# Layer 2's key scores from products of weights and keys; part of these, and the readout's lag products, placed in the wait for the scan

## The reference

```python
q = (hb @ w_q).reshape(PEER_BLOCK, PEER_HEADS, 2, PEER_DHALF)
s = jnp.einsum("nhkd,hkmd->nhkm", q, sub_keys)      # 8 heads, 2 halves, 128 keys
s_half, i_half = lax.top_k(s, PEER_TOPK)
cand = s_half[:, :, 0, :, None] + s_half[:, :, 1, None, :]
top_s, top_c = lax.top_k(cand.reshape(...), PEER_TOPK)
...
g = jax.nn.softmax(top_s, axis=-1)
act = jax.nn.gelu(jnp.einsum("nd,nhkd->nhk", hb, ue))
return jnp.einsum("nhk,nhkd->nd", g * act, ve)
```

## Time and profile before

| | |
|---|---|
| time, median of 3 runs | 3846.15 us (3845.73 to 3854.15) |
| the profiled execution's own time | 3855.96 us |
| its span, from first to last instruction | 3854.2 us |
| PE busy | 3751.7 us, 97% |
| VectorE busy | 2966.6 us, 77% |
| ScalarE busy | 1590.8 us, 41% |
| GpSimd busy | 115.9 us, 3% |
| TensorE's granted clock, mean | 0.99 of full |
| DMA | 669.5 MB, mean 174 GB/s |

### The profile page before, as it was taken

The page is one execution under the profiler, slowest core; times in us unless marked ns, Lnnn a source line. Parts: engine busy times, 40 slices in busy tenths (PEclk is TensorE's granted clock), DMA queues, the critical chain, the costliest instruction groups (busy, mean ns, idle before and its releaser), DMA issues.

```text
span 3854.2 us, 61506 instructions
## 1 busy us (share of the span) xinstructions
PE 3751.7 (97%) x21356; PEld 3172.9 (82%) x21356; DVE 2966.6 (77%) x5358; ACT 1590.8 (41%) x2440; POOL 115.9 (3%) x153
## 2 busy tenths in 40 slices
PE   8999999999999999999999999999989999999998
PEld 7897799556988888888888888888768888888887
DVE  7533275896898899999887899998566997777776
ACT  6301052232137444444484444444332194444443
POOL 0000000000000000000000000000400000000000
PEclk9999999999999999999999999999999999999999
DMA  5314464475422655555515777777735415555554
GB/s 197 104 50 151 145 202 151 162 227 188 164 90 83 204 193 193 197 191 192 188 56 196 239 237 236 239 239 238 171 122 178 161 63 197 189 191 190 191 190 153
DMA packets 204274, 669.52 MB, mean 174 GB/s; under 512 B 36000, under 2 KB 46288, under 8 KB 202592
## 3 DMA queue, kind: packets, MB, share of 16 engines
q1 hardware_dynamic: 159936, 577.31, 45.3%
q0 software_dynamic: 19872, 80.86, 6.8%
q10 hardware_dynamic: 24320, 9.37, 0.9%
HBM read 639.21 MB, written 27.21 MB: 173 GB/s over the span
## 4 chain that ended last, share of the span: by engine, by line
PE 88%; DVE 9%; ACT 1%; DMA 1%; issue 1%; SPq 0%; DVEq 0%; ACTq 0%; POOLq 0%
PE psum L1116 27%; PE psum L1102 16%; PE psum L1104 9%; PE psum L736 5%; PE psum L1195 5%; PE psum L761 4%; PE psum L676 4%; PE psum L1290 3%; PE psum L1081 2%; PE psum L1386 2%; PE psum L1184 2%; DVE arena L2462 1%; DVE arena L2463 1%; PE psum L1161 1%; DVE arena L2464 1%; PE psum L1488 1%
## 5 line engine op out<-in xcount | busy, mean ns | idle before, releaser
L1116 PE MATMUL psum<-v_split,coef_split 128*128 128x512 f32 x4284 | 1034.1, 390 | 0.0
L1102 PE MATMUL psum<-input_split,u_split 128*128 128x512 f32 x2800 | 987.0, 391 | 0.0
L1116 PEld LDWEIGHTS psum<-v_split,coef_split 128*128 128x128 f32 x4284 | 779.7, 188 | 157.1 <-issue 1.2
L1104 PE MATMUL psum<-input_split,u_split 128*128 128x256 f32 x2800 | 788.9, 282 | 0.0
L1102 PEld LDWEIGHTS psum<-input_split,u_split 128*128 128x128 f32 x2800 | 525.3, 188 | 112.7
L1104 PEld LDWEIGHTS psum<-input_split,u_split 128*128 128x128 f32 x2800 | 528.5, 189 | 16.2
L1794 ACT ACTIVATE work<-work 128x256 f32<-128x256 f32 x350 | 146.7, 419 | 851.2 <-DVE work L2604 851.2
L1577 ACT ACTIVATE v_split<-ring 128x1024 fp32r<-128x1024 f32 x357 | 379.7, 1063 | 234.8 <-PE psum L1116 229.0
L2599 DVE TENSOR_TENSOR u_split<-ring,u_split 128x1024 fp32r<-128x1024 f32 x377 | 459.7, 1219 | 12.4 <-ACT u_split L1577 12.4
L2604 DVE TENSOR_REDUCE work<-psum 128x256 f32<-128x512 f32 x350 | 242.1, 692 | 258.8 <-PE psum L1104 257.5
L2599 DVE TENSOR_TENSOR v_split<-ring,v_split 128x1024 fp32r<-128x1024 f32 x357 | 433.9, 1216 | 2.3 <-ACT v_split L1577 2.3
(11 more groups left out here) (466 smaller groups left out, 4722.9 us busy)
## 6 DMA issues: line engine op xcount, KB each, us to landing
ring<-in_u SPq DMA_DIRECT2D x384, 512.0 KB, 3.3
ring<-in_v SPq DMA_DIRECT2D x384, 512.0 KB, 3.3
ring<-in_w SPq DMA_DIRECT2D x324, 512.0 KB, 3.4
arena<-in_ada POOLq DMA_DIRECT2D x48, 512.0 KB, 4.4
scratch_inj<-stage ACTq DMA_DIRECT2D x16, 512.0 KB, 5.2
arena<-scratch_inj POOLq DMA_DIRECT2D x7, 1024.0 KB, 7.8
scratch_cm<-work POOLq DMA_DIRECT2D x8, 512.0 KB, 6.4
scratch_cm<-arena POOLq DMA_DIRECT2D x8, 512.0 KB, 4.9
```

The lines of the kernel that those rows point to most:

```text
L1102: mm(bank(b), rows[:, 0, P * k:P * k + P], HR[:, k, :, :], start=(k == 0), stop=False, skip_group_check=True)
L1104: last = mm(bank(b)[:, 0:S], rows[:, 1, P * k:P * k + P], HR[:, k, 0, :], start=False, stop=(k == 7), skip_group_check=True)
L1116: last = mm(bank(2 + 2 * i + f), CFR[:, b, c, P * i:P * i + P], parts[:, v, 512 * f:512 * f + 512], start=(first and c == 0 and v == 0), s ...
```

## The change: what it does

- The stream has `wk_scan` (12 slots of the transposed query weights) ahead of `ssm_out`, and `wk_last` (20 slots) in place of `q1`. The keys come as one table, `keys2`.
- In the scan wait TensorE makes six "units" (two slots by the keys of one half of a head: 16 products), the units of heads 0 to 2. Of each, ScalarE copies the high part to `WKHO` (in place of `coef_split`) and stores it in HBM; TensorE subtracts it in PSUM (`less_high`: a product with minus the identity, `MINUS`), and ScalarE copies what is left, the low part, to `WKLO` and stores it. There is one buffer for each part. ScalarE's copies of states come behind the six units in its list.
- The readout's 64 lag products come ahead of the wait for "scanned", and `keep_busy(12, 4)` in place of `keep_busy(44, 4)`.
- In `peer_last` the queries and `keys` go. Units 6 and 7 are made ahead of the wait for the split inputs, units 8 to 15 between the scores of heads 1 to 4; the scores are three products of parts, as in layer 1. ScalarE makes both parts of these units (`last_keys`), in three sets of buffers. POOL's queue loads `keys2` and brings the six parked units back, ahead of parking X.
- Fills: 64 and 9 before the builds, then one per build and two at every fourth. ScalarE's copies of the first sums of the experts move from builds 8 and 18 to builds 2 and 12.
- Some semaphores are merged under one name ("exp_args", "rows_made"), with no other effect.

```diff
-                  ("wq", 32), ("ssm_in", 8), ("ssm_out", 16), ("q1", 40)):
+                  ("wq", 32), ("ssm_in", 8), ("wk_scan", 2 * NSCAN), ("ssm_out", 16),
+                  ("wk_last", 32 - 2 * NSCAN)):
...
+            def heads_back(h):
+
+                for kk in range(2):
+                    for part in range(2):
+                        pool.dma_start((LASTL if part else LASTH)[h][:, :, P * kk:P * kk + P].bitcast(F32),
+                                       io["wk"][2 * h + kk, part].rearrange("p (k m) -> p k m", k=KD_))\
+                            .then_inc(sem("wk_back"), 16)
+                pool.wait_ge(sem("wk_back"), 64 * h + 64)
+
+            pool.wait_ge(sem("high_parked"), 16 * NSCAN)
+            pool.wait_ge(sem("low_parked"), 16 * NSCAN)
+            pool.wait_ge(sem("y_summed"), 2)
+            pool.dma_start(KT.rearrange("p n d m -> p (n d m)"), io["keys2"]).then_inc(sem("tables_loaded"), 16)
+            heads_back(0)
+            pool.wait_ge(sem("inputs_scaled"), 5 * KD_ + 1)
+            heads_back(1)
+            heads_back(2)
...
+            def unit(n, keys, off):
+
+                for d in range(2):
+                    arrived(L.slots)
+                    for t in range(8):
+                        last = mm(PS(off + P * t, P), ring[:, L.slots % RING, P * t:P * t + P], keys[:, d, :],
+                                  start=(d == 0 and t % 4 == 0), stop=(d == 1), skip_group_check=True)
+                        if t == 0:
+                            last.then_inc(sem("slot_begun"), 1)
+                    L.slots += 1
+                L.mark(last, "scores_made")
...
+            def less_high(n, high, off):
+
+                pe.wait_ge(sem("wk_copied"), 2 * NH + n + 1)
+                for f in range(2):
+                    last = mm(bank(off // 512 + f), MINUS, high[f], start=False, stop=True, skip_group_check=True)
+                L.mark(last, "scores_made")
...
+                def made(h):
+
+                    for n in (2 * h, 2 * h + 1):
+                        if n >= NSCAN + 2:
+                            pe.wait_ge(sem("wk_low"), 2 * NH + n - 1)
+                        unit(n, KT[:, n], place(n))
+
+                def less(h):
+
+                    for n in (2 * h, 2 * h + 1):
+                        w = LASTH[h % 3][:, :, P * (n % 2):P * (n % 2) + P]
+                        less_high(n, (w[:, 0:4, :], w[:, 4:8, :]), place(n))
+
+                def last_scores(h):
+
+                    if h < NSCAN // 2:
+                        pe.wait_ge(sem("wk_back"), 64 * h + 64)
+                    else:
+                        pe.wait_ge(sem("wk_low"), 2 * NH + 2 * h + 2)
                     if h >= 2:
                         L.take("key_scores_used")
-                    arrived(L.slots)
-                    for k in range(2):
-                        for i in range(2):
-                            for d in range(2):
-                                last = mm(bank(2 + 4 * (h % 2) + i)[:, P * k:P * k + P],
-                                          QT[:, 4 * h + 2 * k + d, P * i:P * i + P],
-                                          ring[:, L.slots % RING, P * (2 * k + d):P * (2 * k + d) + P],
-                                          start=(k == 0 and d == 0), stop=(d == 1), skip_group_check=True)
-                                if k == 0 and i == 0 and d == 0:
-                                    last.then_inc(sem("slot_begun"), 1)
-                    L.slots += 1
+                    for i in range(2):
+                        for k in range(8):
+                            for x, w in ((0, LASTH), (0, LASTL), (1, LASTH)):
+                                last = mm(bank(2 + h % 2)[:, S * i:S * i + S], HR[:, k, x, P * i:P * i + P],
+                                          w[h % 3][:, k, :], start=(i == 0 and k == 0 and not x and w is LASTH),
...
-                for t in range(4 * NH):
-                    pe.wait_ge(sem("lin_free"), l0 + max(t - 1, 0))
-                    arrived(L.slots)
-                    for k in range(8):
-                        if t == 0:
-                            L.take("inputs_shifted")
-                        last = mm(bank(t % 2)[:, 0:S], ring[:, L.slots % RING, k * P:k * P + P], HT[:, k, :],
-                                  start=(k == 0), stop=(k == 7))
-                        if k == 0:
-                            last.then_inc(sem("slot_begun"), 1)
-                    last.then_inc(sem("lin_ready"), 1)
-                    L.slots += 1
-                    if t and t % 4 == 0:
-                        keys(t // 4 - 1)
-                keys(NH - 1)
-                L.lin += 4 * NH
+                pe.wait_ge(sem("tables_loaded"), 128)
+                evacuated()
+                made(3)
+                keep_busy(3, 6)
+                L.take("input_parts")
+                for h in range(NH):
+                    last_scores(h)
+                    if 1 <= h <= 5:
+                        less(h + 2)
+                    if 1 <= h <= 4:
+                        made(h + 3)
                 beside = up_ahead(2)
-                fill(beside, 32)
+                fill(beside, 64)
                 for _ in range(2):
                     L.take("key_scores_used")
-                fill(beside, 12)
                 turn_choice(KK)
                 fill(beside, 9)
                 L.take("chosen_evacuated")
                 for n in range(32):
                     build(64 + n, n % 2, n < 2)
-                    fill(beside, 1 if n % 3 == 2 else 2 if n < 31 else 8)
+                    fill(beside, 2 if n % 4 == 3 else 1)
...
-            keep_busy(44, 4)
+            for n in range(NSCAN):
+                if n >= 2:
+                    pe.wait_ge(sem("wk_low"), 2 * NH + n - 1)
+                pe.wait_ge(sem(f"keys_loaded{n % 2}"), 16 * (n // 2) + 16)
+                unit(n, SCANK[n % 2], 2048 + 1024 * (n % 2))
+                if n:
+                    less_high(n - 1, (WKHO[:, 0:512], WKHO[:, 512:1024]), 2048 + 1024 * ((n - 1) % 2))
+            less_high(NSCAN - 1, (WKHO[:, 0:512], WKHO[:, 512:1024]), 2048 + 1024 * ((NSCAN - 1) % 2))
+            pe.wait_ge(sem("wk_low"), 2 * NH + NSCAN - 1)
+            pe.wait_ge(sem("toep_loaded"), 16 * 32)
+            readout = lambda e, g, j: PS(1024 * e + P * g, P)[NCH * j:NCH * j + NCH, :]
+            for e in range(2):
+                for g in range(8):
+                    for j in range(4):
+                        q = 4 * e + j
+                        mm(readout(e, g, j), UG[:, 8 * q + g, NCH:], TOEP[:, 8 * q + g].rearrange("p t c -> p (t c)"),
+                           start=(g % 4 == 0), stop=False, skip_group_check=True)
+            keep_busy(12, 4)
             L.take("scanned")
...
-                    for part in range(3):
+                    for part in range(2):
                         for j in range(4):
                             q = 4 * e + j
-                            o = PS(1024 * e + P * g, P)[NCH * j:NCH * j + NCH, :]
-                            if part == 0:
-                                mm(o, UG[:, 8 * q + g, NCH:], TOEP[:, 8 * q + g].rearrange("p t c -> p (t c)"),
-                                   start=(g % 4 == 0), stop=False, skip_group_check=True)
-                            else:
-                                last = mm(o, HS[:, :, part - 1, 8 * q + g], BATCHES[8 + q][0][:, g, part - 1, :],
-                                          start=False, stop=(part == 2), skip_group_check=True)
+                            last = mm(readout(e, g, j), HS[:, :, part, 8 * q + g], BATCHES[8 + q][0][:, g, part, :],
+                                      start=False, stop=(part == 1), skip_group_check=True)
...
+            def last_keys(h):
+
+                act.wait_ge(sem("key_scores"), NH + h - 2)
+                for n in (2 * h, 2 * h + 1):
+                    L.take("scores_made")
+                    copy(LASTH[h % 3][:, :, P * (n % 2):P * (n % 2) + P], PS(0 if n % 2 else 2048, 8, P))\
+                        .then_inc(sem("wk_copied"), 1)
+                for n in (2 * h, 2 * h + 1):
+                    L.take("scores_made")
+                    copy(LASTL[h % 3][:, :, P * (n % 2):P * (n % 2) + P], PS(0 if n % 2 else 2048, 8, P))\
+                        .then_inc(sem("wk_low"), 1)
...
+            def scan_unit(n):
+
+                o = 2048 + 1024 * (n % 2)
+                act.wait_ge(sem("scores_made"), 3 * NH + (2 * n if n else 1))
+                if n:
+                    act.wait_ge(sem("high_parked"), 16 * n)
+                copy(WKHO, PS(o, D)).then_inc(sem("wk_copied"), 1)
+                act.wait_ge(sem("wk_copied"), 2 * NH + n + 1)
+                act.dma_start(io["wk"][n, 0], OUTS[0]).then_inc(sem("high_parked"), 16)
+                if n + 2 < NSCAN:
+                    scan_keys(n + 2)
+                act.wait_ge(sem("scores_made"), 3 * NH + min(2 * n + 3, 2 * NSCAN))
+                if n:
```

(6 more changed lines are left out.)

104 lines of the change are left out of this document (51 added, 53 removed).

## The result

The changed kernel takes 3864.92 us in the median of 6 runs (3862.00 to 3868.98), the kernel before 3850.24 in 6 (3845.73 to 3854.15): ratio 1.0037, 95% interval 1.0026 to 1.0047. It is **slower by 0.37%**, some 14 us; the forecast was 3841.3 us in a range to 3856.

A forecast was written before the change was run, and what follows sets the result against it. TensorE was taken to set the time over the whole span, with three waits that matter. Terms -6.8 - 2.9 + 2.0 + 0 + 1.8 + 1.0 = -4.9 us, from 3846.15 to 3841.3 us; likely 3834 to 3848, range 3830 to 3856.

The forecast's parts named there:

- Part 1: Start of layer 2's choice: queries and their scores go, first scores at 2942.8 against 2949.68; -6.8 us.
- Part 2: Heads of the choice: VectorE sets the pace and only its idle goes, 6 gaps of 0.49; -2.9 us.
- Part 3: After the last head: TensorE waits for the chosen keys, then transposes and first build come slower; +2.0 us.
- Part 4: Builds of the gates: twenty fills fewer, 8.7 us of TensorE time, priced at nothing because ScalarE covers it.
- rival B: Builds: ScalarE's 2.65 us only echoes TensorE, so 8.7 us go with the fills; -13.6, 3832.5 us; chance 0.06.
- Part 5: Start of the experts: TensorE idles about 3.3 us and the 96 matmuls run slower; +1.8 us (0 to 2.2).
- Part 7: Readout: lag products are out, the remaining products take 7.0 us, end 2869 against 2868; scan stage +1 us.
- Part 6: Scan wait: further units 6.6 us apart, last low part at 2850.7, "scanned" at 2861.3 instead of 2855.4; +5.9 us.
- POOL's queue: ... covered: POOL's transfers: key table and copies back delay parking X, which is first waited for at 3030; no cost.
- four in a head of 15.1 us are no load: SP's queue in the heads: 32 slots in place of 40, four per head; no cost.
- Rival D: Choice: copies back hold head 1 or unit slots land late, 9.7 us shrink to 1 to 5; 3846 to 3850; chance 0.12.
- Rival C: Scan: TensorE's clock stays at its lower level, +19 in place of +1, total +13, 3859 us; chance 0.10.

The follow-up runs named there:

- e10: Changed kernel with early state copies, three dummies behind the lag products, key tiles ahead of stores, paced loads, six dummies before the turn; ratio 0.9999 to the kernel before.
- e11: As e5, but ten 512 KB stores go out again from a tile nobody writes, so no copy waits for one; scan part 61.68 us.
- e1: Changed kernel with 3 dummy products behind the lag products in place of 12; ratio 1.0042 to the kernel before.
- e8: Changed kernel with 3 dummies and early state copies, plus keys and first head's copies back issued later, at output tiles 8 and 12; output tiles 60.94 us.
- e7: Version with one head (two units) in the scan, with fewer dummies and with keys and first head's copies back issued later; ratio 0.9986 to the kernel before.
- e6: Changed kernel with 3 dummies and early state copies, plus each key tile issued ahead of the high copy and its store; ratio 1.0002 to the kernel before.
- e9: As e7, with keys in eight pieces and the head's copies back one by one, each behind another tile's low part; 3840.82 us, ratio 0.9971.
- e5: Changed kernel with 3 dummies and early state copies, with ten of the twelve stores left out; scan part 51.06 us.

## Why the prediction was wrong

By stages the forecast was -4.9 us and the change cost +11.2. Of these 16.1 us the scan stage with the readout has 12.5 (+13.5, forecast +1.0) and the output tiles 4.2, for which nothing was forecast; the other parts are together 0.6 us better than forecast. The rest of the distance from 3841.3 to 3864.92 us is no fault of any part: the kernel before took 3846.15 us in the median of its first three runs and 3850.24 in that of six (4.1 us), and the medians are 14.7 us apart where the stages give 11.2 (3.5 us, not traced).

**Part 1 (-6.8)** was right: -6.70. **Part 2 (-2.9)**: -2.67. Both to 0.3 us, by layer 1's rows and VectorE's 15.14 us. **Part 3 (+2.0)**: +1.4 in the turn, by the mechanism named, as e10 shows. **Part 4 (0)**: from the first build's start to the last one's end 85.5 us, 85.7 before; rival B falls. **Part 5 (+1.8)**: +1.5, but see the last section. **Part 7**: the readout's remaining products took 7.15 us, 7.0 forecast.

**Part 6 is the step that failed.** It said: "I take 6.6, since the stores lie beside loads as in that row", with the first low part 10.6 us and the last 43.8 us into the stage. They came at 12.9 and 52.4: the first 2.3 late, each further unit 7.9 us on average instead of 6.6. The first was late because not all four slots were there ("The first two units have their weights"): the fourth took 8.61 us to land, and TensorE waited 2.06 us for it. The bound of 6.6 took a store's landing (5.2 us) as fixed, and asked what waits for it. In the stage a high store landed in 7.5 us in the median and a low one in 4.7, and e11 shows that a unit is late even where no copy waits for a store. The bound that came nearest was the one set aside, all traffic over the rate: 48 us at 347 GB/s, against 45 at 374, and even it was 4 us short. It counted 16.8 MB. From the first unit to the last low part 17.8 MB moved, at 340 GB/s on average: GpSimd's batches were 5.7 MB and not four of 1 MB, and only ten stores had landed. Beside the rate there were gaps: a unit whose key tile is late also begins at half clock. The state copies (forecast 10.2 us, measured 10.6) were sized right, only 8.6 us later.

The figure that the prediction cites from the Trainium skill ("DMA: Bandwidth & Descriptors", section "Where 436 GB/s comes from"), 358 GB/s between HBM and SBUF, would have brought the sum 3 us nearer. The six stretches above average 339, under it, with one of 381 above it, as in the earlier trace rows: by this trace it is no ceiling for 10 us, and too high for the mean.

A second term was missing. Part 6 had TensorE ready at 2862 and the states at 2861, about together; with the units late, the last subtraction ended 51.3 us into the stage and not 41.1, the lag products took 5.62 us at the lower clock and not 3.4, and the twelve dummies behind them ended 4.4 us past the last state. I had laid them in as fixed work, where they should have been priced by what happens if the subtraction ahead of them slips. Taking nine of them away (e1) gives back 2.7 us and not 4.4, since the readout then begins at half clock.

**"POOL's queue: ... covered", "four in a head of 15.1 us are no load"** failed as well: +4.2 us in the output tiles. I looked at who waits for the copies back, and not at who shares the queues with them. The key table's 2 MB stand in the same sentence without a price. Rival D named late slots, but at the heads, where they did no harm.

Rival C had the sign and not the cause: 3859 us from a clock stuck at half speed. In the changed kernel the first unit was slow as forecast (5.45 us); of the others only the third was (5.79 in place of 3.81), and then the lag products, after 8.03 us of idle; the level came back each time, in e11 too, where three units began at half clock after 4.2 us of idle each and the fifth, after 1.11 us, ran at the full one.

## What to carry to other kernels

- When a change moves transfers into a wait, add up all bytes of that wait first, with those in flight when it begins, and divide by the rate that a long full stretch keeps, gaps included, and not by that of the fullest short one: here 340 GB/s over 52 us, with 10 us stretches of 282 to 381. 17.8 MB do not fit into 48.5 us at that rate, and at 374 they seem to. Four units fitted here, six did not.
- A load that is early enough can still be in the way. Paced behind the consumer's own progress, the same 4 MB cost 0 us that cost 2.5 to 6 us as two bursts (e8, e7).
- Dummy products are work on the path as soon as what stands before them is late. Give their number by where they must end: too few, and the products behind them begin at half clock (e1: 4.4 us gained, 1.7 lost).

## What the runs showed of the hardware that I had not expected

- A small load is as slow as what stands ahead of it: 128 KB issued right behind a 512 KB store landed after 10.10 us; issued ahead of the store (e6), the third unit started 3.2 us sooner.
- Stores that nobody waits for hold the units up as well: scan part 61.68 us, 60.57 with the waits and 51.06 without the stores. By the ratios they cost less than waited ones (7 and 12 us), and the intervals do not settle it.
- The start of the experts has two values that do not follow from the idle ahead of it. With the same 3.15 us of idle the 96 matmuls took 24.18 us in the changed kernel and 22.62 in e9:

```profile
3151.18 22.62 PE L1150 MATMUL psum<-u_split,coef_split 128*128 128x512 f32 x96 [3.15 <-DVE u_split L2689]
```

  Of the kernels with that idle, eight show 24.1 to 24.2 and four 22.6. What decides was not tried. In the same way the turn took 7.4 to 7.6 us in e5 and e8 and 6.2 to 6.5 in the other six-unit kernels without e10's dummies; no run explains it.
- What stays open: the scan part scattered by 2.4 us between two kernels alike up to its end (changed and e1), and e10's ratio shows some 5 us less than its stages. The runs of one kernel here are 5 to 15 us apart, so a single profile against a median can differ by as much. e5's profile is its fastest run, 8 us under its median, and e11's is near its slowest. Whether six units would fit with the key tiles ahead of the stores and a second pair of buffers stays open too.
